# Expert query panels as three products of rounded operands, and the last searches moved beside the U blocks

## The chip, the cores and the metric

The kernel runs on one core of one Trainium2 chip. The metric is device time in microseconds (us); the kernel before has a median of 2666.05 us over three runs (2664.07 to 2666.25).

## The reference, cut to what matters

Two blocks are applied to x (256 tokens, 1024 wide). The second has two layers, and each ends with an expert layer, `peer`. Everything is float32.

```python
def peer(h, w_q, subkeys, u_tab, v_tab):             # 8 heads, 128 keys a side, top 16, 128*128 experts
    q = (xb @ w_q).reshape(128, 8, 256)
    s1 = einsum('phd,nd->phn', q[..., :128], subkeys[0])
    s2 = einsum('phd,nd->phn', q[..., 128:], subkeys[1])
    v1, i1 = top_k(s1, 16);  v2, i2 = top_k(s2, 16)
    cand = v1[..., :, None] + v2[..., None, :]       # 256 candidates a head
    cs, ci = top_k(cand, 16);  g = softmax(cs)
    e = i1[ci // 16] * 128 + i2[ci % 16]
    a = gelu(einsum('pd,phkd->phk', xb, u_tab[e]))
    return einsum('phk,phkd->pd', g * a, v_tab[e])
```

xb is the normed and modulated activation, `rmsnorm(x, g) * (1 + scale) + shift`.

## The kernel before, in words

Activations lie transposed: features on the partitions in 8 blocks (`KT`) of 128, the 256 tokens as columns. Weights come through a ring of four 1 MB slots (`ring`), one panel per slot, in the order of `SECTIONS`. SyncE issues each load (`load`, L343) once the panel that used the slot before is done with, counted on the semaphore which the section names.

An expert layer (`peer` on each engine) has these stages.

**The norm.** The 4 panels of the projection before it make 8 tiles; VectorE adds each to `xT` (`residual`, L1543), ScalarE squares it (L1036), TensorE sums the squares (`norm`, L483). After the root, VectorE scales the 8 blocks (L1534) and ScalarE adds the shift (L1048), which gives `hP`. ScalarE then rounds all of `hP` to float32r (L1075, `h_split[0]`) and VectorE computes the rest (L1630, `h_split[1]`).

**The query stage.** There are 8 panels of `peer_wq`, one per head. For each head TensorE makes two tiles (the two key sides) of 8 float32 products, weights straight from the ring (`proj_cols`, L499), and ScalarE copies each tile to `qT` (`evac`, L1029). Banks 4 and 5 alternate. One head later TensorE multiplies that head's `qT` with the subkeys (`keys`, L618) into one of banks 0 to 3, and VectorE searches them: `pick(h, tt)`, for each half of the tokens, finds the 16 best of 128 for both key sides (`first8`, `next8`, L1641 to L1661). `keys` of head h waits until the search that used its bank before has let go of it. `keys` of head 7 comes after the first U block; its two searches come in the passes b = 2 and 3 of VectorE's loop over the blocks.

**The U blocks.** All 16384 experts' U rows are multiplied with the activation, in 128 blocks (`BLOCKS`) of 128 experts. ScalarE rounds a block (`hi_u`, L1088) and VectorE computes the rest (`lo`, L1729), both into `t_split`, which lies over ring slots 2 and 3; the U panels (two blocks each) use slots 0 and 1. TensorE makes three products for each of the 8 feature blocks (`hidden`, L637): rounded by rounded, rounded by rest, rest by rounded. Only the last 8 of the 24 need VectorE's part. ScalarE rounds block b once block b-2 has been multiplied; the slot of a panel is loaded again once VectorE has finished its second block (semaphore `split`, L369).

Beside the blocks VectorE ranks the candidates in steps (`rank`): for each half of the tokens four pairs of `cand` (sums, first 8) and `rest` (next 8), `place`, six `where`, `gates`. A table written from sizes puts them at passes b: they begin at `FIRST` = 4 and spread over `SPAN` = 45 blocks. From `HOT_AT` = FIRST + SPAN + 6 = 55 each of 64 passes makes one-hot rows for four tokens, TensorE multiplies them (`gates`, L649), and from `GATE_AT` = 57 ScalarE and VectorE merge the result with the block outputs in the arena.

**The V blocks.** The same number of blocks, with products of 512 columns (L678).

Three lines fix the places that the change touches (L252, L297, L306):

```python
queries = [(a["peer_wq"][l], 8, "proj", 2)]
H_PEER = (5, 8)
FIRST, SPAN = 4, 45
```

Of the kernel before, what the change touches and what calls it, by code (L numbers as in the profile page):

```python
# [14 lines left out]
D, T, P, KT = 1024, 256, 128, 8  # L15
# [3 lines left out]
RING = 4  # L19
SLOT = 2048  # L20
EXPERTS, PH, TOPK = 16384, 8, 16
# [89 lines left out]
def build(nc, a, out):  # L111
# [4 lines left out]
    with ctx:  # L116
# [40 lines left out]
        def slot(n):  # L157
            return ring[:, n % RING, :]
# [10 lines left out]
        def kt(ap, k=KT):  # L169
# [9 lines left out]
                  "mod_acc", "mod_turn", "mod_bank", "proj", "turn", "bank4", "bank5", "sq", "ms", "var", "std", "h",  # L179
                  "h_hi", "h_split", "hi", "split", "lb", "gate", "gates_f", "logf", "expo", "exps", "lin_in",  # L180
                  "scores", "masked", "dstate", "state", "o_sum", "o_bank0", "o_bank1", "osq", "oms", "ovar", "ostd",
# [69 lines left out]
        def peer_sections(l):  # L251
            queries = [(a["peer_wq"][l], 8, "proj", 2)]  # L252
            return queries + [((a["peer_u"][l], a["peer_v"][l]), 2 * PAIRS, None, 0)]
# [25 lines left out]
        for dram, panels, signal, _ in SECTIONS:  # L279
            if dram is a["w_down"]:  # L280
                DOWN += range(n, n + panels)
            n += panels if signal is not None else 0

        LOADS_BEFORE, PROJ_BEFORE, loads, n = [], [], [0, 0], 0
        projs = 0
        for _, panels, signal, per in SECTIONS:
            projs += panels * per * (signal == "proj") + 2 * PAIRS * (signal is None)
# [41 lines left out]
        def _(sync):  # L329
# [5 lines left out]
            n, freed, layer = 0, [], 0  # L335
            total = {"proj": 0, "mod_acc": 0, "rows": 0}
            at = {}
# [12 lines left out]
            for dram, panels, signal, per in SECTIONS:  # L350
                if signal is not None:
                    k0 = at.get(id(dram), 0)
                    at[id(dram)] = k0 + panels
                    for k in range(panels):
                        total[signal] += per
                        freed.append((signal, total[signal]))
                        load(dram[k0 + k])
                    continue
# [54 lines left out]
        def _(pe):  # L413
# [186 lines left out]
            def peer(l):  # L600
# [40 lines left out]
                def gates(g):  # L641
# [8 lines left out]
                    last.then_inc(sems["g_mm"], 1)  # L650

                for h in range(PH):
                    proj_cols(1, lambda k: hP[:, k, :], T, first=(h == 0))
                    if h:
                        keys(h - 1, 3)
                pe.wait_ge(sems["h_split"], l + 1)
                for b in range(BLOCKS):
                    for tt in range(2):
                        if b == STEP_AT[tt, "gates", 0] + 2:
                            turn_routes(tt)  # L660
                    hidden(b % 2)
                    if b == 0:
                        keys(PH - 1, 2)
                    g = group_of(b, HOT_AT)
                    if g is not None:
                        gates(g)
# [350 lines left out]
        def _(act):  # L1017
# [54 lines left out]
            def peer(l, scale_col, shift):  # L1072
                norm(xT, hP, shift, "proj")
                act.wait_ge(sems["h"], H_PEER[l] * KT)
                A(h_split[:, 0, :, :], hP, ACT.Copy).then_inc(sems["h_hi"], 1)  # L1075
                qT = M5["qT"].rearrange("p (s t) -> p s t", s=16)
# [45 lines left out]

                def squares(g):
# [16 lines left out]
                for b in range(1, BLOCKS + 2):  # L1140
# [12 lines left out]
                    if g is not None:  # L1153
                        squares(g)
                    if b >= 2:
# [303 lines left out]
        def _(dve):  # L1459
# [79 lines left out]

            def residual(name, gate, mods_behind=()):  # L1540
                for k in range(KT):
                    bank, free = ring_tile(name)
                    STT(xT[:, k, :], bank[:, 0:T], modc[:, gate + k:gate + k + 1], xT[:, k, :], MUL, ADD).then_inc(free, 1)  # L1543
                    if k in mods_behind:
                        used(1)
                        mod_between(1, 16)
                dve.wait_ge(*e.tile_out())

# [75 lines left out]
            iota16 = iota[:, 0:16].unsqueeze(1).broadcast_to([P, P, 16])  # L1624

            def peer(l):
# [25 lines left out]
                def next8(rows):  # L1652
# [7 lines left out]
                    ins.then_inc(sems["dve_step"], 1)  # L1660
                    e.step()  # L1661

                def pick(h, tt):
# [109 lines left out]
                for b in range(BLOCKS + 3):  # L1773
                    if 2 <= b < BLOCKS:
# [449 lines left out]
            e.tiles("turn", 16)  # L2224
            residual("proj", 16)
            used(8)
# [112 lines left out]
```

## Time and profile before

| | |
|---|---|
| median of 3 runs | 2666.05 us |
| profiled execution, own time | 2666.74 us |
| its span, first to last instruction | 2664.9 us |
| around the span | 1.84 us |
| TensorE busy | 2585.9 us (97%) |
| VectorE busy | 1712.7 us (64%) |
| ScalarE busy | 1172.0 us (44%) |
| mean granted TensorE clock | 0.975 of 2.4 GHz |

Times of trace rows are in us from the start of the span. A float32 product is recorded as two instructions, so a tile of 8 such products shows 16; a product of float32r operands is one. Layer 0's query stage lies between 771 and 834 us, layer 1's between 1795 and 1860. A wait in brackets is the idle time of the engine before the row, with what ended it.

### The profile page before, as it was taken

The numbers are of one execution on the slowest core, as the hardware profiler recorded it, in microseconds if no ns is written. First come the engines' busy times: TensorE is split into PE (matmuls) and PEld (weight loads), VectorE is DVE, ScalarE is ACT, GpSimd is POOL, SyncE is SP. The second block draws the span as 40 slices with busy tenths as digits, with TensorE's granted clock in tenths as the row PEclk, the third lists the DMA queues.
The fourth block names the chain that finished last, engine by engine and source line by source line (L and its number), as shares of the span: only waits on it lengthen the run. The fifth ranks groups of instructions, "written<-read, shape, count | busy, mean of one in ns | idle before, by whom it ended". The sixth has DMA issues, their size and how long they took to land.

```text
span 2664.9 us, 41646 instructions
## 1 busy us (share of the span) xinstructions
PE 2585.9 (97%) x15364; PEld 2286.4 (86%) x15364; DVE 1712.7 (64%) x3469; ACT 1172.0 (44%) x2355; POOL 3.5 (0%) x10
## 2 busy tenths in 40 slices
PE   8999999999999999999999998999999999999997
PEld 4588888897889999999888887778999999888886
DVE  3662644446438977787688875536996778555554
ACT  2322010124212558776444444231557777455554
POOL 0000000000000000000000000000000000000000
PEclk9999999998999999999999999779999999999998
DMA  6562557754433554444677764212554444555553
GB/s 257 189 238 84 204 190 264 253 175 163 169 127 119 185 178 148 137 141 158 242 274 274 281 235 148 79 64 97 175 188 159 143 143 137 180 190 196 196 189 110
DMA packets 65346, 471.60 MB, mean 177 GB/s; under 512 B 7297, under 2 KB 7553, under 8 KB 8241
## 3 DMA queue, kind: packets, MB, share of 16 engines
q1 hardware_dynamic: 64656, 467.85, 50.0%
q8 instruction: 101, 1.65, 0.3%
q10 hardware_dynamic: 272, 1.05, 0.1%
q0 software_dynamic: 272, 0.69, 0.1%
q14 instruction: 45, 0.36, 0.0%
HBM read 468.51 MB, written 1.05 MB: 176 GB/s over the span
## 4 chain that ended last, share of the span: by engine, by line
PE 94%; DVE 4%; ACT 1%; issue 1%; DMA 1%; SPq 0%; DVEq 0%
PE bank L637 26%; PE bank L678 26%; PE bank L499 16%; PE bank L649 4%; PE bank L744 4%; PE bank L828 2%; PE bank L509 2%; PE bank L934 2%; PE bank L483 1%; PE bank L445 1%; PE bank L891 1%; DVE macc L1501 1%; PE bank L515 1%; PE bank L742 1%; PE bank L469 1%
## 5 line engine op out<-in xcount | busy, mean ns | idle before, releaser
L637 PE MATMUL bank<-h_split,t_split 128*128 128x256 f32 x6144 | 771.7, 285 | 4.5 <-DVE t_split L1729 4.2
L637 PEld LDWEIGHTS bank<-h_split,t_split 128*128 128x128 f32 x6144 | 745.4, 191 | 6.5 <-DVE t_split L1729 5.2
L1729 DVE TENSOR_TENSOR t_split<-ring,t_split 128x1024 fp32r<-128x1024 f32 x512 | 624.9, 1222 | 159.0 <-ACT t_split L1088 155.3
L678 PE MATMUL bank<-t_split,w_split 128*128 128x512 f32 x3072 | 703.9, 390 | 0.0
L678 PEld LDWEIGHTS bank<-t_split,w_split 128*128 128x128 f32 x3072 | 574.9, 188 | 118.7
L1093 ACT ACTIVATE t_split<-ring 128x1024 fp32r<-128x1024 f32 x256 | 271.7, 1061 | 357.9 <-PE bank L678 282.9
L1088 ACT ACTIVATE t_split<-ring 128x1024 fp32r<-128x1024 f32 x256 | 271.1, 1059 | 298.3 <-PE bank L637 264.8
L1029 ACT ACTIVATE arena<-bank 128x256 f32<-128x256 f32 (+2 forms) x160 | 64.4, 405 | 482.1 <-PE bank L499 292.4
L499 PE MATMUL bank<-H,ring 128*128 128x256 f32 (+1 forms) x960 | 246.9, 419 | 6.4 <-ACT H L1048 4.0
L1761 DVE TENSOR_TENSOR w_split<-arena,w_split 128x256 fp32r<-128x256 f32 x256 | 108.9, 425 | 223.1 <-ACT w_split L1095 223.1
L499 PE MATMUL bank<-arena,ring 128*128 128x256 f32 x1024 | 231.0, 385 | 12.2 <-ACT arena L1048 8.0
L499 PEld LDWEIGHTS bank<-H,ring 128*128 128x128 f32 x960 | 186.0, 195 | 61.1 <-issue 36.9
L499 PEld LDWEIGHTS bank<-arena,ring 128*128 128x128 f32 x1024 | 195.6, 193 | 40.7 <-issue 9.4
L1501 DVE SCALAR_TENSOR_TENSOR macc<-ring,cact,macc 128x256 f32<-128x256 f32 x336 | 162.9, 485 | 12.0
L1095 ACT ACTIVATE w_split<-arena 128x256 fp32r (+1 forms) x256 | 102.7, 401 | 0.0
L744 PE MATMUL bank<-H,ring 128*128 128x256 f32 x448 | 100.5, 381 | 0.3 <-DVE macc L1994 0.3
L744 PEld LDWEIGHTS bank<-H,ring 128*128 128x128 f32 x448 | 83.8, 190 | 11.8 <-issue 0.5
L1817 DVE SCALAR_TENSOR_TENSOR macc<-arena,cact,macc 128x256 f32<-128x256 f32 x168 | 81.1, 483 | 3.4
L1114 ACT ACTIVATE arena<-bank 128x256 f32<-128x256 f32 (+31 forms) x236 | 75.0, 318 | 0.1
L828 PE MATMUL bank<-hf_split,wd_split 128*128 128x256 f32 x528 | 66.4, 290 | 3.8 <-DVE wd_split L2043 3.8
L828 PEld LDWEIGHTS bank<-hf_split,wd_split 128*128 128x128 f32 x528 | 65.8, 198 | 4.0 <-DVE wd_split L2043 4.0
L1543 DVE SCALAR_TENSOR_TENSOR xT<-bank,modc,xT 128x256 f32<-128x256 f32 x40 | 18.8, 483 | 76.7 <-PE bank L499 64.6
(290 smaller groups left out, 2380.7 us busy)
## 6 DMA issues: line engine op xcount, KB each, us to landing
ring<-in_peer_u SPq DMA_DIRECT2D x128, 1024.0 KB, 5.0
ring<-in_peer_v SPq DMA_DIRECT2D x128, 1024.0 KB, 4.9
ring<-in_w_mod SPq DMA_DIRECT2D x24, 1024.0 KB, 5.1
ring<-in_mod_w SPq DMA_DIRECT2D x24, 1024.0 KB, 5.0
arena<-in_mod_w SPq DMA_DIRECT2D x24, 1024.0 KB, 6.6
ring<-in_w_in SPq DMA_DIRECT2D x22, 1024.0 KB, 5.0
ring<-in_w_up SPq DMA_DIRECT2D x22, 1024.0 KB, 5.1
ring<-in_peer_wq SPq DMA_DIRECT2D x16, 1024.0 KB, 4.9
```

Source lines behind the costliest of these rows:

```text
L499: last = mm(bank[:, 0:width], w[:, k, j * P:(j + 1) * P], rhs(k), start=(k == 0), stop=(k == ks - 1))
L637: last = mm(bank[:, 0:T], u[:, a_, k, :], h_split[:, b_, k, :], start=(k == 0 and a_ + b_ == 0), stop=(k == KT - 1 and a_ == 1))
L649: last = mm(BK[6 + b][:, j * P:(j + 1) * P], P2[b][:, j, :], P1[b][:, j, :], start=True, stop=True)
L678: last = mm(BK[2 * tt + hf][:, :], w_split[:, j, a_, tt * P:(tt + 1) * P], t_split[:, 1 - j, b_, hf * 512:(hf + 1) * 512], start=(first an ...
L744: last = mm(bank[:, 0:T], w[:, k, half], Hx[:, k, :], start=(k == 0), stop=(k == KT - 1))
L828: return mm(BK[d // 2][:, d % 2 * T:(d % 2 + 1) * T], w[:, j, d * P:(d + 1) * P], hf_split[:, b_, 2 * n + j, :], start=(n == j == a_ == b_ ...
L1088: A(t_split[:, 1 - j, 0, :].rearrange("p (k c) -> p k c", k=KT), ring[:, r, :].rearrange("p (k j c) -> p j k c", k=KT, j=2)[:, j], ACT.Cop ...
L1093: A(t_split[:, 1 - j, 0, :].rearrange("p (k c) -> p k c", k=KT), ring[:, r, :].rearrange("p (j k c) -> p j k c", k=KT, j=2)[:, j], ACT.Cop ...
L1095: A(w_split[:, j, 0, :], arena[:, bass.ds(at * T, T)], ACT.Copy).then_inc(sems["w_hi"], 1)
L1501: ins = STT(acc, w[:, k, :], cact[:, c_col + k:c_col + k + 1], acc, MUL, ADD)
L1729: TT(t_split[:, 1 - j, 1, :].rearrange("p (k c) -> p k c", k=KT), ring[:, r, :].rearrange(view, k=KT, j=2)[:, j], t_split[:, 1 - j, 0, :]. ...
L1761: TT(w_split[:, b % 2, 1, :], arena[:, bass.ds(at * T, T)], w_split[:, b % 2, 0, :].bitcast(f32), SUB).then_inc(sems["w_ready"], 1)
```

## The change

The query panels of both layers are handled as the U blocks are. ScalarE rounds each panel in two halves (`hi_q`), VectorE computes the rest in two halves (`lo_q`), both into `q_split`, a double buffer at the start of the arena, and TensorE makes three products (`query`). The ring slot is free once `lo_q` has read it. The rounding of the activation moves into the norm's last step: ScalarE's shift writes `h_split[0]`, and VectorE computes `h_split[1]` block by block. The rounding of heads 0 and 1 is done during the projection before the norm. `keys` of head 6 moves behind U block 0, that of head 7 behind U block 5; the searches of heads 5, 6 and 7 are cut into twelve quarters (`quarter`: one key side of one half of the tokens), one in each of the passes b = 1 to 12, and the ranking starts at block 13 and is spread over 43 blocks. `FIRST, SPAN = 13, 43` puts `HOT_AT` at 62 and `GATE_AT` at 64. In `part(j, a_, b_, ...)`, j is the tile, a_ = 1 takes the panel's rest and b_ = 1 the activation's.

```diff
-            queries = [(a["peer_wq"][l], 8, "proj", 2)]
+            queries = [(a["peer_wq"][l], PH, "q_lo", 1)]
...
+        q_split = nc.alloc_sbuf_tensor_at("q_split", [P, 2, 2, SLOT], f32r, offset=arena_at)
+        AHEAD = PH - 3
-        H_PEER = (5, 8)
+        H_PEER = (4, 7)
-        FIRST, SPAN = 4, 45
+        FIRST, SPAN = 13, 43
...
 # TensorE, peer
+                def query(h):
+                    w = q_split[:, h % 2, :, :].rearrange("p s (k c) -> p s k c", k=KT)
+                    banks = []
+                    def part(j, a_, b_, first, last_one):
+                        if first:
+                            banks.append(ring_bank())
+                        for k in range(KT):
+                            if h == j == a_ == 0:
+                                fresh(k, 1, "h_lo" if b_ else "h")
+                            last = mm(banks[j][:, 0:T], w[:, a_, k, j * P:(j + 1) * P], h_split[:, b_, k, :],
+                                      start=(first and k == 0), stop=(last_one and k == KT - 1))
+                        if last_one:
+                            last.then_inc(sems["proj"], 1)
+                    pe.wait_ge(sems["q_hi"], 2 * (PH * l + h + 1))
+                    if h == 0:
+                        pe.wait_ge(sems["q_lo"], PH * l + 1)
+                        for j in range(2):
+                            part(j, 0, 0, True, False)
+                            part(j, 1, 0, False, False)
+                        for j in range(2):
+                            part(j, 0, 1, False, True)
+                    else:
+                        for j in range(2):
+                            part(j, 0, 0, True, False)
+                            part(j, 0, 1, False, False)
+                            if j == 0:
+                                pe.wait_ge(sems["q_lo"], PH * l + h + 1)
+                            part(j, 1, 0, False, True)
...
                 for h in range(PH):
-                    proj_cols(1, lambda k: hP[:, k, :], T, first=(h == 0))
-                    if h:
+                    query(h)
+                    if 1 <= h <= AHEAD + 1:
                         keys(h - 1, 3)
-                pe.wait_ge(sems["h_split"], l + 1)
                 for b in range(BLOCKS):
...
                     if b == 0:
-                        keys(PH - 1, 2)
+                        keys(PH - 2, 4)
+                    if b == 5:
+                        keys(PH - 1, 7)
 # ScalarE, peer
-                norm(xT, hP, shift, "proj")
-                act.wait_ge(sems["h"], H_PEER[l] * KT)
-                A(h_split[:, 0, :, :], hP, ACT.Copy).then_inc(sems["h_hi"], 1)
+                def hi_q(h):
+                    m = QUERY[l][h]
+                    act.wait_ge(sems[f"loaded{m % RING}"], 16 * (m // RING + 1 + (PAIRS * l if m % RING < 2 else 0)))
+                    for j in range(2):
+                        half = slice(j * D, (j + 1) * D)
+                        A(q_split[:, h % 2, 0, half], slot(m)[:, half], ACT.Copy).then_inc(sems["q_hi"], 1)
+                if l == 0:
+                    act.wait_ge(sems["o_done"], 1 + 8)
+                hi_q(0)
+                hi_q(1)
+                squares(xT, hP, "proj")
+                std_root()
+                for k in range(KT):
+                    act.wait_ge(sems["hs"], e.more("hs"))
+                    A(h_split[:, 0, k, :], hP[:, k, :], ACT.Identity, bias=modc[:, shift + k:shift + k + 1]).then_inc(sems["h"], 1)
...
+                        act.wait_ge(sems["q_lo"], PH * l + 6)
                         hi_u(0)
                     evac("proj", qT[:, s, :], ACT.Copy)
+                    if s % 2 and s // 2 + 2 < PH:
+                        hi_q(s // 2 + 2)
+                act.wait_ge(sems["q_lo"], PH * (l + 1))
 # VectorE, peer
-                dve.wait_ge(sems["h_hi"], e.more("h_hi"))
-                TT(h_split[:, 1, :, :], hP, h_split[:, 0, :, :].bitcast(f32), SUB).then_inc(sems["h_split"], 1)
+                for k in range(KT):
+                    dve.wait_ge(sems["h"], H_PEER[l] * KT + k + 1)
+                    STT(h_split[:, 1, k, :], hP[:, k, :], modc[:, 24 + k:25 + k], h_split[:, 0, k, :].bitcast(f32), ADD, SUB
+                        ).then_inc(sems["h_lo"], 1)
...
-                for h in range(PH - 2):
+                lo_q(l, 2)
+                for h in range(AHEAD):
+                    lo_q(l, h + 3)
                     for tt in range(2):
                         pick(h, tt)
-                for tt in range(2):
-                    lo(0, tt, "p (k j c) -> p j k c")
-                    pick(PH - 2, tt)
+                lo(0, 0, "p (k j c) -> p j k c")
...
-                    if b in (2, 3):
-                        pick(PH - 1, b - 2)
+                    if b <= 12:
+                        quarter(AHEAD + (b - 1) // 4, (b - 1) // 2 % 2, (b - 1) % 2)
 # VectorE, the residual before each expert layer
-            residual("proj", 16)
+            residual("proj", 16, (), {5: lambda: lo_q(0, 0), 6: lambda: lo_q(0, 1)})
```

The loop over the blocks on VectorE now begins at b = 1 with `lo` of block 1 (before, `lo` of blocks 0 and 1 stood between the searches of head 6). `quarter` does `first8` and `next8` for one row set, and lets go of the bank after its second key side.

## Rows read from the trace of the kernel before

**Rows 1.** The page: busy time, and the chain that ended last, by line

```profile
PE 2585.9 (97%) x15364; PEld 2286.4 (86%) x15364; DVE 1712.7 (64%) x3469; ACT 1172.0 (44%) x2355; POOL 3.5 (0%) x10
PE bank L637 26%; PE bank L678 26%; PE bank L499 16%; PE bank L649 4%; PE bank L744 4%; PE bank L828 2%; PE bank L509 2%; PE bank L934 2%; PE bank L483 1%; PE bank L445 1%; PE bank L891 1%; DVE macc L1501 1%; PE bank L515 1%; PE bank L742 1%; PE bank L469 1%
```

**Rows 2.** Timeline, all engines: norm and first two heads; columns start, us, engine

```profile
763.45 0.48 DVE L1543 SCALAR_TENSOR_TENSOR xT<-bank,modc,xT 128x256 f32<-128x256 f32 x1 [2.97 <-PE bank L499]
769.67 3.26 DVE L1534 SCALAR_TENSOR_TENSOR arena<-xT,gain,nrm 128x256 f32<-128x256 f32 x8
770.19 3.30 ACT L1048 ACTIVATE arena<-arena,modc 128x256 f32<-128x256 f32 x8 [2.34 <-DVE arena L1534]
770.84 15.49 PE L499 MATMUL bank<-arena,ring 128*128 128x256 f32 x64 [3.98 <-ACT arena L1048]
...
1795.40 16.90 PE L499 MATMUL bank<-arena,ring 128*128 128x256 f32 x64 [3.98 <-ACT arena L1048]
```

**Rows 3.** Windows around that start: PE, PEld, DVE, ACT, POOL busy, then granted clock

```profile
772.00:773.00 1.00, 1.00 (x4) 0.82 (x3) 0.92 (x3) 1.00 (x4) 0.00 (x0) 0.50 0.00 0
774.00:775.00 1.00, 1.00 (x7) 0.87 (x6) 0.00 (x0) 1.00 (x1) 0.00 (x0) 1.00 0.00 0
1800.00:1801.00 1.00, 1.00 (x4) 0.82 (x3) 0.97 (x1) 0.00 (x0) 0.00 (x0) 0.50 0.00 0
```

**Rows 4.** Timeline, layer 0, one head of the query stage in its steady part

```profile
817.37 1.05 PE L618 MATMUL bank<-small,arena 128*128 128x128 f32 x8
818.01 0.50 DVE L1644 MAX8 arena<-bank 128x8 f32<-128x128 f32 x2 [2.17 <-PE bank L618]
820.80 0.48 DVE L1644 MAX8 arena<-bank 128x8 f32<-128x128 f32 x2
821.91 0.38 ACT L1029 ACTIVATE arena<-bank 128x256 f32<-128x256 f32 x1 [3.96 <-PE bank L499]
825.17 1.05 PE L618 MATMUL bank<-small,arena 128*128 128x128 f32 x8
```

**Rows 5.** Timeline of ScalarE, steady U blocks: the rounding of two successive blocks

```profile
866.77 1.06 ACT L1088 ACTIVATE t_split<-ring 128x1024 fp32r<-128x1024 f32 x1 [1.55 <-PE bank L637]
869.65 1.06 ACT L1088 ACTIVATE t_split<-ring 128x1024 fp32r<-128x1024 f32 x1 [1.55 <-PE bank L637]
```

**Rows 6.** Timeline of TensorE, first U blocks of layer 0

```profile
833.78 3.12 PE L637 MATMUL bank<-h_split,t_split 128*128 128x256 f32 x24
...
849.36 3.13 PE L637 MATMUL bank<-h_split,t_split 128*128 128x256 f32 x24 [0.78 <-DVE t_split L1729]
853.99 46.21 PE L637 MATMUL bank<-h_split,t_split 128*128 128x256 f32 x381 [1.50 <-DVE t_split L1729]
```

**Rows 7.** Windows of the U blocks, columns as in Rows 3

```profile
845.00:857.00 12.00, 9.73 (x77) 9.12 (x77) 11.76 (x40) 3.99 (x6) 0.00 (x0) 1.00 0.42 133
857.00:869.00 12.00, 12.00 (x103) 12.00 (x102) 11.79 (x34) 5.32 (x8) 0.00 (x0) 1.00 0.62 220
1872.00:1884.00 12.00, 10.11 (x82) 9.70 (x81) 11.79 (x37) 3.99 (x6) 0.00 (x0) 1.00 0.51 171
```

**Rows 8.** Timeline of VectorE among the ranking steps

```profile
864.98 1.23 DVE L1729 TENSOR_TENSOR t_split<-ring,t_split 128x1024 fp32r<-128x1024 f32 x1
866.12 0.75 DVE L1685 TENSOR_TENSOR arena<-arena 128x256 f32<-128x256 f32 x2
869.40 1.23 DVE L1729 TENSOR_TENSOR t_split<-ring,t_split 128x1024 fp32r<-128x1024 f32 x1
871.95 0.75 DVE L1655 MAX8 arena<-arena 128x8 f32<-128x256 f32 x2
873.62 1.23 DVE L1729 TENSOR_TENSOR t_split<-ring,t_split 128x1024 fp32r<-128x1024 f32 x1
```

**Rows 9.** Groups by line, VectorE, 846 to 983 us: a `where` step

```profile
L1710 DVE TENSOR_TENSOR arena<-arena,con 128x2048 f32<-128x2048 f32 x4 | 9.1, 2286 | 0.0
```

**Rows 10.** The page: DMA issues, KB each, us from issue to landing

```profile
ring<-in_peer_u SPq DMA_DIRECT2D x128, 1024.0 KB, 5.0
```

More of the change, by code:

```diff
@@ L282, in build @@
             n += panels if signal is not None else 0
+        QUERY, n = [], 0
+        for _, panels, signal, _ in SECTIONS:
+            if signal == "q_lo":
+                QUERY.append(range(n, n + panels))
+            n += panels if signal is not None else 0
         LOADS_BEFORE, PROJ_BEFORE, loads, n = [], [], [0, 0], 0
@@ L286, in build @@
         for _, panels, signal, per in SECTIONS:
-            projs += panels * per * (signal == "proj") + 2 * PAIRS * (signal is None)
+            projs += panels * (2 if signal == "q_lo" else per * (signal == "proj")) + 2 * PAIRS * (signal is None)
             if signal is None:
@@ L335, in _ @@
             n, freed, layer = 0, [], 0
-            total = {"proj": 0, "mod_acc": 0, "rows": 0}
+            total = {"proj": 0, "mod_acc": 0, "rows": 0, "q_lo": 0}
             at = {}
@@ L355, in _ @@
                         total[signal] += per
+                        if signal == "q_lo":
+                            total["proj"] += 2
                         freed.append((signal, total[signal]))
@@ L650, in gates @@
                     last.then_inc(sems["g_mm"], 1)
+                def query(h):
[26 more added lines that the diff above has]
+                            part(j, 1, 0, False, True)
+                    e.skip(f"loaded{panel[0] % RING}", 16)
+                    panel[0] += 1
                 for h in range(PH):
-                    proj_cols(1, lambda k: hP[:, k, :], T, first=(h == 0))
-                    if h:
+                    query(h)
+                    if 1 <= h <= AHEAD + 1:
                         keys(h - 1, 3)
-                pe.wait_ge(sems["h_split"], l + 1)
                 for b in range(BLOCKS):
@@ L1121, in stored, with offsets @@
                       ).then_inc(sems["g_store"], 1)
-                def squares(g):
+                def offsets(g):
                     if g >= 2:
@@ L1153, in peer @@
                     if g is not None:
-                        squares(g)
+                        offsets(g)
                     if b >= 2:
@@ L1538, in norm, with residual @@
                     ins.then_inc(sems["h"], KT)
-            def residual(name, gate, mods_behind=()):
+            def residual(name, gate, mods_behind=(), also={}):
                 for k in range(KT):
@@ L1546, in residual @@
                         mod_between(1, 16)
+                    if k in also:
+                        also[k]()
                 dve.wait_ge(*e.tile_out())
@@ L1624, in _, with lo_q @@
             iota16 = iota[:, 0:16].unsqueeze(1).broadcast_to([P, P, 16])
+            def lo_q(l, h):
+                for j in range(2):
+                    half = slice(j * D, (j + 1) * D)
+                    dve.wait_ge(sems["q_hi"], 2 * (PH * l + h) + j + 1)
+                    ins = TT(q_split[:, h % 2, 1, half], slot(QUERY[l][h])[:, half], q_split[:, h % 2, 0, half].bitcast(f32), SUB)
+                ins.then_inc(sems["q_lo"], 1)
             def peer(l):
@@ L1661, in next8, with quarter @@
                     e.step()
+                def quarter(h, tt, half):
+                    n = 2 * h + tt
+                    bank, free = BK[n % 4], sems[f"rank_bank{n % 4}"]
+                    dve.wait_ge(sems["ranked"], RANKS * l + n + 1)
+                    rows = [(bank[:, half * P:(half + 1) * P], s2[:, half * P:(half + 1) * P],
+                             topv[:, tt, h, half, :], topi[:, tt, h, half, :])]
+                    if half:
+                        first8(rows).then_inc(free, 1)
+                        dve.wait_ge(free, (5 if n % 4 < 2 else 4) * l + n // 4 + 1)
+                    else:
+                        first8(rows).then_inc(sems["dve_step"], 1)
+                        dve.wait_ge(sems["dve_step"], e.stepped())
+                    next8(rows)
                 def pick(h, tt):
@@ L1765, in peer @@
                 used(8)
-                for h in range(PH - 2):
+                lo_q(l, 2)
+                for h in range(AHEAD):
+                    lo_q(l, h + 3)
                     for tt in range(2):
                         pick(h, tt)
-                for tt in range(2):
-                    lo(0, tt, "p (k j c) -> p j k c")
-                    pick(PH - 2, tt)
+                lo(0, 0, "p (k j c) -> p j k c")
                 e.tiles("proj", 16)
-                for b in range(BLOCKS + 3):
-                    if 2 <= b < BLOCKS:
+                for b in range(1, BLOCKS + 3):
+                    if b < BLOCKS:
                         lo(b // 2 % 2, b % 2, "p (k j c) -> p j k c")
-                    if b in (2, 3):
-                        pick(PH - 1, b - 2)
+                    if b <= 12:
+                        quarter(AHEAD + (b - 1) // 4, (b - 1) // 2 % 2, (b - 1) % 2)
                     if b >= 3:
@@ L2224, in _ @@
             e.tiles("turn", 16)
-            residual("proj", 16)
+            residual("proj", 16, (), {5: lambda: lo_q(1, 0), 6: lambda: lo_q(1, 1)})
             used(8)
```

2 lines of the change are left out of this document (1 added, 1 removed).

## The prediction

> **What bounds the kernel now.** I read the page first: TensorE is busy 97% of the span, and of the chain that ended last 16% is float32 products of L499, the line that the query panels use too [rows 1]. So time is saved only where TensorE has less to do or stands less. Then the timelines of the stage. A tile of 8 float32 products takes 3.45 us (a residual row and the wait before it, 0.48 + 2.97) [rows 2], so a panel of two takes 6.90. From one head's `keys` to the next is 825.17 - 817.37 = 7.80 us, so `keys` costs 0.90. In that period VectorE needs 2 x 2.79 = 5.6 us for two searches (from one MAX8 to the next) and waits 2.17 us [rows 4]. The stage runs from 770.84 [rows 2] to the first U block at 833.78 [rows 6], 62.9 us; in layer 1 the first four tiles take 1.4 us longer [rows 2]. In the U blocks TensorE goes on without a gap, one block of 24 products every 869.65 - 866.77 = 2.88 us, 0.120 us a product [rows 5]. It stands only near the start, where VectorE is late with `lo` [rows 6]: in the 12 us of the first window 77 products begin where the undisturbed window has 103, in layer 1's worst window 82 [rows 7]. At 0.120 us that is 3.1 and 2.5 us lost.
>
> **TensorE's query panels.** 48 products of 0.120 us are 5.76 us a panel, where 6.90 go; the operands and shapes are those of a U block. The bounds for the price of a product are 0.117 (12 us by the 103 of the full window [rows 7]) and 0.130 (3.12 by 24, which holds a drain [rows 6]). Seven panels save 7 x 1.14 = 8.0 us a layer.
>
> The first panel is special. The activation's blocks come 0.41 us apart (3.30 by 8) and ScalarE has written the last 2.65 us after TensorE starts (773.49 - 770.84) [rows 2]. The first tile's 8 products go at that pace, and nothing behind them may pass; with a hand-over and the last product at the low clock they end at 3.1 us, and the panel takes 3.1 + 40 x 0.120 = 7.9 us. Before, the first two panels took 15.49 us, the first thus 8.6 [rows 2]. TensorE has stood 3.98 us for the norm and begins at a clock of 0.50; it is 1.00 by 774 in layer 0, while layer 1 still has 0.50 at 1800 [rows 3], 4.6 us after its start. I let the clock return at the same moments: nothing more in layer 0, and half of 2.6 us, 1.3, in layer 1, against 1.4 before. The first panel thus gives 0.7, and 0.8 in layer 1.
>
> **The other engines in the stage.** ScalarE's rounding of a panel is 2 x 1.06 us [rows 5] and follows the evacuation of the head two earlier, so it is done 2.6 us after that head's end; TensorE needs it 6.65 us after it. VectorE's `lo` takes 1.14 us until the next instruction starts (866.12 - 864.98) [rows 8], a panel 2.28, and with two searches 7.86 us a head. TensorE's head is 5.76 + 0.90 = 6.66. VectorE is thus the slower one and falls 1.2 us behind per head; moving three heads' searches out is what ends that. Counted from the end of head 1's products: the rest of panel 3 is done at 2.6 + 1.1 = 3.7, then one search pair and one panel each 7.86, so panels 4 to 7 at 11.6, 19.4, 27.3, 35.1. TensorE starts head h at 0.9 + 6.66 (h - 2) and wants the rest after 16 products, 1.9 later: 16.1, 22.8, 29.4, 36.1. The spare falls to 1.0 us at head 7. Head 7 ends at 0.9 + 33.3 + 5.8 = 40.0; U block 0 wants `lo` at 41.9 and has it at 35.1 + 5.6 + 1.2 = 41.9. Nothing is lost, and 0.2 us more a head on VectorE would cost up to 1. What a bank holds back (`keys` of head 5 needs the searches of head 3) is free by 33, before 34.
>
> The stage thus lasts 7.9 + 5.8 + 40.0 = 53.7 us, 9.2 less than 62.9. One `keys` (0.90) has moved into the U blocks and comes off: **8.3 us in layer 0, 8.4 in layer 1**.
>
> **What I cost at nothing.** `hi_q` of heads 0 and 1 lies ahead of the squares on ScalarE: panel 1 lands some 5 us [rows 10] after the second projection panel is free, with four tiles still to come, and 8 squares catch up before TensorE wants them. If that cover went, the norm would be late by what is missing, up to 2 us. `lo_q` of heads 0 and 1 is 2.28 us in VectorE's waits of 2.97 [rows 2]; it fits. VectorE's parts of the activation follow ScalarE's block by block and are wanted only after 32 products. The removed full-width roundings lay beside TensorE's work. Ring loads start earlier than before, since a slot is free at `lo_q`; the first U panels wait for heads 5 to 7, 5 us before they are used at the latest.
>
> **The U blocks.** A quarter is half of a 2.79 us search, 1.4, to 2.8 if the halves shared everything; I take 1.5, because only the hand-overs between dependent steps are shared. With `lo` that is 2.65 us per block against TensorE's 2.88, and TensorE has two `keys` more there: VectorE starts even and stays so. Before, it started with three searches owed, which gave the 3.1 and 2.5 us; those go. Next late is the ranking. It is denser: `cand` 3.28 (869.40 - 866.12) and `rest` 1.67 (873.62 - 871.95) [rows 8] four times, six `where` of 2.3 [rows 9], and some 2 for the rest make 35.7 us per half, 71.4 over 43 blocks, 1.66 a block; with `lo` 2.80 against 2.88. And the table puts `cand`, `rest`, `cand` at blocks 13, 14 and 15: 3 x 1.14 + 8.4 = 11.9 us in 8.6. The debt of 3.2 meets an ease of 2.4 (`lo` is normally done 1.1 + 1.2 us after the previous block's start and wanted at 2.88 + 1.92, so 2.4 later): 0.9 us lost per layer, with 0 to 3 as bounds. The last gates come at block 125 instead of 118, and V's first rounding waits for them; TensorE has blocks 126 and 127 meanwhile, so 0, up to 1.
>
> **Sum.** 8.3 + 8.4 + (3.1 + 2.5) - 2 x 0.9 = 20.5 us. Against the profiled execution's 2666.74 this gives 2646.2; it lies 0.7 above the median of 2666.05, which gives **2645.5**.
>
> **Rivals.**
> (A) The forecast: 60%.
> (B) VectorE becomes the bound in the query stage: a panel and two searches cost 8.5 instead of 7.86 (contention, a hand-over before each `lo_q`). For it: a spare of only 1.0 us at head 7. Against: all its parts have rows. Four heads late by 0.6 and the same debt at blocks 0 to 5 cost 2.5 to 5 us per layer: 2651 to 2655. 17%.
> (C) The clock returns later in the first panel, because its products come 0.41 us apart and leave TensorE waiting between them where float32 products at the low clock filled it. If all of a first panel's 40 remaining products ran at 0.50, that is 4.8 us a layer, less 1.3: up to 8.3, so 2649 to 2654. For it: layer 1 kept the low clock 4.6 us at full work [rows 3]. 13%. The Trainium skill (TensorE: Matmul & The Clock Gate, Part 1) calls the halved clock the resting state, which activity releases; by that rule thin work keeps it low.
> (D) The other side: a product pays its weight load in the open. 48 loads a panel take the place of 32 instructions (two per float32 product). Nearest row: a key instruction with 128 columns costs 0.90 / 8 = 0.11 us. At 0.120 + 0.11 a panel is 11 us and 768 products add 85: 2730. It decides from 0.120 + 20.5 / 768 = 0.147 us a product. Against it stand the U blocks with the same form at 0.120 [rows 5]. 4%. The Trainium skill (the same page, Part 3, The mechanism) says a weight load overlaps with running matmuls only when its row group differs; every load here takes all rows, so by that rule D would hold, and rows 5 speak against it.
> (E) The change does not do what it says, since the early waits and the ranking give back what the panels save (a U panel that lands late in each pair of blocks of the denser ranking, 0.2 us a block over 43 blocks and two layers is 17 us): about 2662. For it: VectorE at 97% there. 6%.
>
> **How the numbers follow.** About 0.2%, 5.3 us, is what a measurement of this kernel tells from no change. A, B and C are faster by more, E partly: faster 0.93; within: 0.03; slower, D and a bad E: 0.04. The range takes A with its bounds (0.117 a product gives 2 us more, no ranking stall 1.8 more, clock in layer 1 1 more: 2640) and B and C up to 2655.
>
> **What would show it.** Query products at 0.120 us, heads 6.66 us apart, first U block some 53.7 us after the first query product. VectorE waits of 2.17 us before searches gone, its `lo` of panel 7 about 1 us before TensorE wants it. No TensorE wait in blocks 1 to 12, one of about 1 us near block 16. Low clock gone by the same moments. I am wrong in the main step if a head's products take over 6.2 us, in VectorE's if TensorE waits for `lo_q`, and in the U blocks if waits for VectorE there add to more than 4 us a layer.

## The result, and the profile after

The changed kernel takes 2643.72 us (median of 4 runs, 2640.44 to 2647.02) where the kernel before takes 2666.15 (4 runs): a ratio of 0.9916, 95% interval 0.9897 to 0.9934. The forecast was 2645.5 and the range 2639 to 2655. The profiled execution took 2647.02 us with a span of 2645.2, 19.7 less than the span of before.

The page of the changed kernel: busy time, the chain that ended last by engine and by line, and the new group of query products.

```profile
PE 2566.3 (97%) x15620; PEld 2281.5 (86%) x15620; DVE 1751.9 (66%) x3501; ACT 1194.1 (45%) x2385; POOL 3.5 (0%) x10
PE 89%; DVE 8%; ACT 1%; issue 1%; DMA 0%; DVEq 0%; SPq 0%
PE bank L724 26%; PE bank L647 26%; PE bank L509 11%; PE bank L659 4%; PE bank L790 4%; PE bank L874 2%; PE bank L519 2%; PE bank L980 2%; PE bank L674 1%; DVE macc L1565 1%; PE bank L455 1%; PE bank L937 1%; PE bank L493 1%; PE bank L525 1%; DVE q_split L1697 1%
L674 PE MATMUL bank<-h_split,q_split 128*128 128x256 f32 x768 | 101.3, 293 | 8.0 <-ACT h_split L1135 8.0
```

TensorE is as full as before (97%, [rows 1]) and has less to do. Float32 products (now L509) fell from 16% of the chain to 11%, and VectorE's work on `q_split` has come in with 1%. The two waits of L674, 8.0 us in all, are those for the norm.

The same line by engine, in the page of the kernel before:

```profile
PE 94%; DVE 4%; ACT 1%; issue 1%; DMA 1%; SPq 0%; DVEq 0%
```

VectorE's share of the chain has doubled, from 4% to 8%.

The timeline of TensorE in layer 0 of the changed kernel: start, us, then the group; in brackets a wait.

```profile
770.06 15.35 PE L674 MATMUL bank<-h_split,q_split 128*128 128x256 f32 x96 [3.98 <-ACT h_split L1135]
785.25 1.05 PE L628 MATMUL bank<-small,arena 128*128 128x128 f32 x8
...
791.75 1.05 PE L628 MATMUL bank<-small,arena 128*128 128x128 f32 x8
...
818.54 5.88 PE L674 MATMUL bank<-h_split,q_split 128*128 128x256 f32 x48
824.26 2.08 PE L647 MATMUL bank<-h_split,t_split 128*128 128x256 f32 x16
827.09 1.22 PE L647 MATMUL bank<-h_split,t_split 128*128 128x256 f32 x8 [0.76 <-DVE t_split L1820]
...
876.00 24.26 PE L647 MATMUL bank<-h_split,t_split 128*128 128x256 f32 x200 [0.81 <-DVE t_split L1820]
```

Against [rows 4] the heads are 6.50 us apart (791.75 - 785.25), not 7.80. Less the 0.89 of `keys` (a `keys` group starts 0.89 us before the products behind it in the timeline with float32 panels below), a panel's 48 products take 5.61 us, 0.117 each. Against [rows 6] the waits for VectorE in the U blocks have moved from blocks 4 to 6 to block 0 (0.76) and block 16 (0.81).

Where the time went can be added up from the first query product, the first U product and the first V product of the two executions:

| us | before | after | difference |
|---|---|---|---|
| layer 0, query stage | 62.94 | 54.20 | -8.74 |
| layer 0, U blocks | 430.27 | 430.11 | -0.16 |
| layer 1, query stage | 64.35 | 54.55 | -9.80 |
| layer 1, U blocks | 430.27 | 430.05 | -0.22 |

That is 18.9 of the 19.7 us of the spans. Layer 0's stage begins 0.8 us earlier, which is not the work of the new panels: it does so too in x1 below, with float32 panels (770.02). The stretch from layer 0's V blocks to layer 1's first query product differs by 1 us one way, the end by 1 us the other. The differences of the U blocks are no larger than those between two executions of the changed kernel (430.11 and 430.51 us in layer 0).

The first head is the odd one. It ends at 785.25 less a panel of 5.61, so it took 9.6 us, and the granted clock says why. Windows of the changed kernel, columns as in [rows 3]:

```profile
772.00:774.00 2.00, 2.00 (x9) 1.78 (x8) 2.00 (x6) 0.71 (x2) 0.00 (x0) 0.50 0.00 0
776.00:777.00 1.00, 1.00 (x7) 1.00 (x7) 0.00 (x0) 0.00 (x0) 0.00 (x0) 0.50 0.00 0
778.00:779.00 1.00, 1.00 (x11) 1.00 (x10) 0.00 (x0) 0.09 (x1) 0.00 (x0) 1.00 0.00 0
1792.00:1793.00 1.00, 1.00 (x6) 1.00 (x6) 0.00 (x0) 0.00 (x0) 0.00 (x0) 0.50 0.00 0
1795.00:1797.00 2.00, 2.00 (x19) 2.00 (x18) 0.00 (x0) 0.61 (x2) 0.00 (x0) 1.00 0.00 0
```

Before, the 2.4 GHz were back by 774 in layer 0 [rows 3]; now, with the stage beginning 0.8 us earlier, 776 still shows 0.50 (1.2 GHz), and the clock is back 7 to 8 us after the first query product in both layers. Six or seven products begin in 1 us at 0.50, eleven at 1.00.

### The profile page after: what moved, and what is told of

Read it like the earlier page. It is cut to its first block, busy times and chain, and to the rows that moved or that the text cites. A ratio compares the mean times of both kernels' runs of the same rounds, so it can differ in the third digit from the quotient of the medians.

```text
span 2645.2 us, 42222 instructions
## 1 busy us (share of the span) xinstructions
PE 2566.3 (97%) x15620; PEld 2281.5 (86%) x15620; DVE 1751.9 (66%) x3501; ACT 1194.1 (45%) x2385; POOL 3.5 (0%) x10
## 3 DMA queue, kind: packets, MB, share of 16 engines
q10 hardware_dynamic: 272, 1.05, 0.1%
HBM read 468.51 MB, written 1.05 MB: 178 GB/s over the span
## 4 chain that ended last, share of the span: by engine, by line
PE 89%; DVE 8%; ACT 1%; issue 1%; DMA 0%; DVEq 0%; SPq 0%
PE bank L724 26%; PE bank L647 26%; PE bank L509 11%; PE bank L659 4%; PE bank L790 4%; PE bank L874 2%; PE bank L519 2%; PE bank L980 2%; PE bank L674 1%; DVE macc L1565 1%; PE bank L455 1%; PE bank L937 1%; PE bank L493 1%; PE bank L525 1%; DVE q_split L1697 1%
## 5 line engine op out<-in xcount | busy, mean ns | idle before, releaser
L1075 ACT ACTIVATE arena<-bank 128x256 f32<-128x256 f32 (+2 forms) x160 | 64.3, 405 | 451.7 <-PE bank L509 194.4
L509 PE MATMUL bank<-H,ring 128*128 128x256 f32 (+1 forms) x960 | 244.6, 416 | 6.5 <-ACT H L1094 4.0
L509 PEld LDWEIGHTS bank<-H,ring 128*128 128x128 f32 x960 | 185.0, 194 | 59.6 <-issue 35.7
L509 PE MATMUL bank<-arena,ring 128*128 128x256 f32 x512 | 113.7, 381 | 4.2 <-DVE H L2108 2.2
L509 PEld LDWEIGHTS bank<-arena,ring 128*128 128x128 f32 x512 | 96.3, 190 | 18.3 <-DVE H L2108 3.0
L674 PE MATMUL bank<-h_split,q_split 128*128 128x256 f32 x768 | 101.3, 293 | 8.0 <-ACT h_split L1135 8.0
L674 PEld LDWEIGHTS bank<-h_split,q_split 128*128 128x128 f32 x768 | 97.0, 197 | 10.5 <-issue 8.7
L1178 ACT ACTIVATE arena<-bank 128x256 f32<-128x256 f32 (+32 forms) x250 | 79.9, 320 | 0.1
```

What stands on the lines that cost most here:

```text
L509: last = mm(bank[:, 0:width], w[:, k, j * P:(j + 1) * P], rhs(k), start=(k == 0), stop=(k == ks - 1))
L674: last = mm(banks[j][:, 0:T], w[:, a_, k, j * P:(j + 1) * P], h_split[:, b_, k, :], start=(first and k == 0), stop=(last_one and k == KT - 1))
```

## The experiments

**One part each.** The first kernel has the searches, `keys` and ranking of the changed one and the panels of the one before. The second is the reverse.

```diff
 # x1, from the kernel before
-        FIRST, SPAN = 4, 45
+        FIRST, SPAN = 13, 43
...
+                    if b <= 12:
+                        quarter(AHEAD + (b - 1) // 4, (b - 1) // 2 % 2, (b - 1) % 2)
 # x2, from the changed kernel
-        FIRST, SPAN = 13, 43
+        FIRST, SPAN = 4, 45
...
-                for h in range(AHEAD):
-                    lo_q(l, h + 3)
+                for h in range(PH - 2):
+                    if h + 3 < PH:
+                        lo_q(l, h + 3)
```

> The searches, keys and ranking placed as in the changed kernel, the query panels still float32 products and rounding of the activation as before. My theory (the panels' products carry the gain, moving searches alone buys only the removed waits at the first U blocks): stage about 62.0 us from the first query product to the first U block (62.9 less one keys), waits for VectorE in the U blocks 0.8 us a layer instead of 2.3, one keys more there; in all 1.5 us a layer, 2663 us. Rival (VectorE was what held the stage, so moving searches is the gain): heads under 7.8 us apart and 2655 us or less.

> The three products, with the searches of heads 5 to 7 and the ranking placed as in the kernel before. My theory (VectorE with 7.8 us a head against TensorE's 6.5 then becomes the bound at the end of the stage): heads still 6.5 us apart, but U block 0 waits about 4.7 us for VectorE, and 2.3 us more are lost in blocks 3 to 6; 5.4 us a layer above the changed kernel, about 2654 us. Rival (the ring and the banks have ease enough, VectorE's debt is hidden): within 2 us of the changed kernel, 2644 to 2646 us.

Measured: x1 takes 0.9988 of the kernel before (0.9979 to 0.9998, 2661.75 against 2665.16 us), x2 takes 0.9989 (0.9979 to 0.9998, 2661.69). The timeline of TensorE in x1, then in x2:

```profile
825.89 1.05 PE L619 MATMUL bank<-small,arena 128*128 128x128 f32 x8
826.78 7.07 PE L500 MATMUL bank<-arena,ring 128*128 128x256 f32 x32
833.50 3.21 PE L638 MATMUL bank<-h_split,t_split 128*128 128x256 f32 x24
...
884.40 20.80 PE L638 MATMUL bank<-h_split,t_split 128*128 128x256 f32 x171 [0.81 <-DVE t_split L1747]
```

```profile
816.70 5.90 PE L674 MATMUL bank<-h_split,q_split 128*128 128x256 f32 x48
823.42 2.15 PE L647 MATMUL bank<-h_split,t_split 128*128 128x256 f32 x16
830.78 2.08 PE L647 MATMUL bank<-h_split,t_split 128*128 128x256 f32 x8 [5.22 <-DVE t_split L1818]
832.66 1.91 PE L628 MATMUL bank<-small,arena 128*128 128x128 f32 x8
```

x1 went as my theory had it: with float32 panels VectorE's searches, 5.6 us a head [rows 4], are hidden (heads stay 7.80 us apart), and what changes is the waits in the U blocks, to one of 0.81 for VectorE near block 16 (layer 1 has another, of 1.21, for ScalarE). Its stages of 63.48 and 63.38 us are 1.4 above my figure, since the clock was back only after 6 us in both. x2 went further than both theories. The panels are as fast as in the changed kernel (stages of 54.97 and 54.84 us with one `keys` more), but U block 0 waits 5.2 us for VectorE, and the U blocks last 437.9 and 438.4 us, 7.8 and 8.4 more than the changed kernel's. In layer 0 the rows give (5.22 + 0.38 + 1.49) - (0.76 + 0.81) - 0.89 for the `keys` that is not there = 4.6 of the 7.8. Most of the other 3.2 is what the wait does to the clock, which my 5.4 lacked: TensorE runs at 0.50 for 5.7 us behind the wait, which costs half of that, 2.8. Windows of x2:

```profile
826.00:828.00 2.00, 0.00 (x0) 0.00 (x0) 1.93 (x13) 0.00 (x0) 0.00 (x0) 1.00 0.00 0
830.00:831.00 1.00, 0.22 (x1) 0.22 (x2) 1.00 (x3) 0.00 (x0) 0.00 (x0) 0.50 0.00 0
834.00:835.00 1.00, 1.00 (x6) 1.00 (x6) 1.00 (x3) 1.00 (x1) 0.14 (x1) 0.50 0.00 0
```

TensorE stands, the clock falls to 0.50, and the `keys` behind the wait take 1.91 us instead of 1.05. So a wait of 5.2 us there costs about 8. Alone, the two parts bring 3.4 and 3.5 us, where both together bring 22 (19 in the repeat below): each makes the other worth having.

**The first head.** Two edits on the changed kernel. The fill gives TensorE four products with each block of the activation instead of one. The warm-up puts nine float32 products of constants into its wait for the norm; their result is used by nothing.

```diff
 # x3: the fill
-                        for j in range(2):
-                            part(j, 0, 0, True, False)
-                            part(j, 1, 0, False, False)
+                        banks += [ring_bank(), ring_bank()]
+                        for k in range(KT):
+                            fresh(k, 1, "h")
+                            for j in range(2):
+                                for a_ in range(2):
+                                    mm(banks[j][:, 0:T], w[:, a_, k, j * P:(j + 1) * P], h_split[:, 0, k, :],
+                                       start=(k == a_ == 0), stop=False)
 # x5: the warm-up
+        WARM = 9
...
                 norm(hP)
+                for _ in range(WARM):
+                    mm(BK[3][:, 0:T], ones, C("scan_g"), start=True, stop=True)
```

> Head 0's products are reordered: with each block of the activation as it comes, four products (both tiles, rounded and rest of the panel) instead of one. Theory thin work (the clock comes back late in the changed kernel because TensorE waits between its first products): the clock is back 3 to 6 us after the first product instead of 7 to 7.7, and head 0 takes 7.4 to 8.5 us instead of 9.7; 1.5 to 2.3 us a layer, about 2640 us. Rival theory chance (the moment at which the clock returns is not tied to how thin the first products are): it is back 7 us after the first product as now, and only the filled waits are saved, 0.5 to 1 us a layer, about 2642 us.

> Nine float32 products of constants (result unused) fill TensorE's 4 us wait for the norm ahead of each query stage. If the halved clock in head 0 comes from that wait: granted clock 1.00 from the first query product, head 0 takes 7.5 us instead of 9.7 to 10, 2.2 to 2.5 us a layer gained, about 2639 us. If the clock falls for another reason, or the fill makes the first query product late: clock still 0.50 or head 0 unchanged, 2644 us or more.

Windows of x3, then of x5, in layer 0 and layer 1:

```profile
771.00:773.00 2.00, 2.00 (x11) 2.00 (x11) 2.00 (x7) 2.00 (x6) 0.00 (x0) 0.50 0.67 283
774.00:775.00 1.00, 1.00 (x11) 1.00 (x10) 1.00 (x4) 0.00 (x0) 0.00 (x0) 1.00 0.00 0
1784.00:1785.00 1.00, 1.00 (x11) 1.00 (x10) 1.00 (x4) 0.00 (x0) 0.00 (x0) 0.99 0.00 0
```

```profile
771.00:773.00 2.00, 1.94 (x6) 0.93 (x5) 2.00 (x6) 2.00 (x7) 0.00 (x0) 1.00 0.76 320
774.00:776.00 2.00, 2.00 (x12) 2.00 (x11) 2.00 (x6) 0.00 (x0) 0.00 (x0) 0.50 0.03 8
1791.00:1793.00 2.00, 2.00 (x20) 2.00 (x19) 1.24 (x4) 0.00 (x0) 0.00 (x0) 1.00 0.00 0
```

In x3 the stages begin at 770.58 and 1779.95, so the clock is back 3 to 4 us after the first product, not 7; the stages last 51.71 and 52.15 us, 2.5 and 2.4 less than the changed kernel's. In x5 the clock is up when the stage begins (770.81), but in layer 0 it falls at about 774, after 3 us in which TensorE got one product with each block of the activation; in layer 1 it stays up. The stages last 53.79 and 52.37 us. The medians of these two cannot tell this (2643.51 and 2644.51 us, 4 runs each, which spread over 4 to 6 us); the traces can. Between the two stages the executions differ by as much as the edits bring: from layer 0's first V product to layer 1's first query product x3's took 527.1 us and the changed kernel's 532.4. In one of two stages thin work lowered the clock with no long wait before it.

**Two waits on VectorE.** The rest of U block 0 goes ahead of the last search, and the table's `cand` size becomes 36.

```diff
-                 for p in range(4) for part, size in (("cand", 33), ("rest", 18))]
+                 for p in range(4) for part, size in (("cand", 36), ("rest", 18))]
...
                     for tt in range(2):
+                        if h == AHEAD - 1 and tt == 1:
+                            lo(0, 0, "p (k j c) -> p j k c")
                         pick(h, tt)
-                lo(0, 0, "p (k j c) -> p j k c")
```

> The rest of U block 0 is taken ahead of the last search of the stage, and the ranking table is given a cand size of 36, so that its first steps fall in blocks 13, 15 and 16 instead of 13, 14 and 15. My theory (both waits of TensorE in the changed kernel's U blocks are order on VectorE, 0.76 at block 0 and 0.81 at block 16): both gone, U stage 1.5 us shorter in each layer, 2641 us. Rival (VectorE is at its limit there and the waits come back a few blocks later): waits of the same sum at other blocks, 2644 us.

Measured: 2640.06 us (4 runs, 2636.09 to 2645.44, too wide a spread to show a gain of this size). Both waits are gone in both layers; the timeline of TensorE in layer 0 shows one stretch from block 6 to block 31, across block 16:

```profile
824.48 3.03 PE L647 MATMUL bank<-h_split,t_split 128*128 128x256 f32 x24
...
843.43 75.34 PE L647 MATMUL bank<-h_split,t_split 128*128 128x256 f32 x624
919.13 8.89 PE L647 MATMUL bank<-h_split,t_split 128*128 128x256 f32 x72 [0.36 <-ACT arena L1178]
```

The U blocks last 428.81 and 429.10 us, 1.3 and 1.0 less. A wait for ScalarE's evacuation has come in near block 32 (0.36, and 0.66 in layer 1). ScalarE itself had stood 3.4 us for a U panel that landed late. Timelines of x6, VectorE and ScalarE:

```profile
903.42 1.23 DVE L1820 TENSOR_TENSOR t_split<-ring,t_split 128x1024 fp32r<-128x1024 f32 x1
906.88 1.22 DVE L1820 TENSOR_TENSOR t_split<-ring,t_split 128x1024 fp32r<-128x1024 f32 x1
...
917.75 1.06 ACT L1148 ACTIVATE t_split<-ring 128x1024 fp32r<-128x1024 f32 x1 [3.37 <-DMA ring<-in_peer_u]
918.71 0.36 ACT L1178 ACTIVATE arena<-bank 128x256 f32<-128x256 f32 x1
```

Beside the `where` steps VectorE's rests start 3.46 us apart, against TensorE's 2.88 a block, and a slot is loaded again only when VectorE has read it. So both theories hold in part, mine for the larger one: 0.36 of 1.57 us (0.66 of 1.51 in layer 1) came back some blocks later, by way of the ring. That VectorE's pace is what made this panel late is read from the rows; no run changed it.

**Fill and warm-up together, and all four.**

> The filled start of head 0 and the constants' products in the norm's wait, together. Theory thin work (the clock falls or stays low when TensorE's first products are thin, with or without a wait before them): granted clock 1.00 through all of head 0 in both layers, 5.6 to 5.9 us for its 48 products, first U block 50 us after the first query product instead of 54.4; 8 to 9 us less than the changed kernel in the two stages, about 2635 us. Theory wait alone (the fall in layer 0 of the kernel with the fill alone was chance of the moment): the clock falls again in one of the layers, 51 to 53 us there.

> All four edits: filled start, constants' products in the norm's wait, rest of block 0 ahead of the last search, cand size 36. If they add: 50 us from first query product to first U block, no waits for VectorE in the U blocks, 12 us less than the changed kernel, about 2632 us. If VectorE becomes the bound with the shorter head 0: waits for the panels' rest at heads 6 and 7 and 2636 us or more.

x7 takes 2637.08 us (4 runs). Its clock is 1.00 throughout the first head in both layers, and its stages last 51.09 us both times. Windows and timeline of x7:

```profile
772.00:774.00 2.00, 2.00 (x17) 2.00 (x18) 2.00 (x7) 2.00 (x6) 0.00 (x0) 1.00 0.86 365
1784.00:1786.00 2.00, 2.00 (x20) 2.00 (x19) 2.00 (x6) 2.00 (x5) 0.00 (x0) 1.00 0.55 225
```

```profile
771.98 3.98 PE L690 MATMUL bank<-h_split,q_split 128*128 128x256 f32 x32
775.79 8.42 PE L677 MATMUL bank<-h_split,q_split 128*128 128x256 f32 x64
784.05 1.05 PE L631 MATMUL bank<-small,arena 128*128 128x128 f32 x8
```

My 50 us missed one wait. The first 32 products are done by 775.8, and the last 16 want VectorE's rest of the activation, which comes until 777.2 (it starts at 773.98 in x7 and takes 3.26 us). Head 0 thus takes 6.5 us (784.05 - 5.61 - 771.98), not 5.7. The two stages are 6.6 us shorter than the changed kernel's, where I had expected 8 to 9. x8 has stages of 51.11 and 51.13 us and U blocks of 429.17 and 429.95; together that is 7.5 us less than in the changed kernel, not 12, and 1.5 less than in x7. It takes 2639.2 us (6 runs, 2630.8 to 2641.5), which does not tell it from x7, and misses the 2632 of adding up. No panel's rest is waited for at heads 6 and 7, so VectorE did not become the bound.

**VectorE's spare.**

```diff
                         pick(h, tt)
+                    dve.memset(M5["eq"][:, 0:256], 0.0)
```

> VectorE writes 256 unused zeros after the searches of each of the five heads in the stage (0.2 to 0.3 us a head more). By the changed kernel's trace VectorE's rest of panel 7 is done 0.1 us before TensorE wants it, so the spare is gone: TensorE waits for it at head 6 or 7, together with block 0's wait 1.0 to 1.5 us a layer more than the changed kernel's 0.76. If the spare is the 1.0 us of the prediction: no wait for a panel's rest, and block 0 waits 1.0 us longer all the same.

The timeline of x9 at head 7:

```profile
814.10 0.27 DVE L1862 MEMSET arena<- 128x256 f32 x1
814.29 2.29 DVE L1697 TENSOR_TENSOR q_split<-ring,q_split 128x1024 fp32r<-128x1024 f32 x2
...
816.63 4.04 PE L674 MATMUL bank<-h_split,q_split 128*128 128x256 f32 x32 [0.65 <-DVE q_split L1697]
```

With 0.19 us a head more (814.29 - 814.10) TensorE waits 0.65 us for the rest of panel 7, and 0.94 at block 0, 1.6 us in all against 0.76 (1.64 against 0.71 in layer 1). Five heads by 0.19 is 0.95; 0.83 came through (0.93 in layer 1), a little under the 1.0 that I had expected. The kernel was run once, 2644.53 us, which says nothing against the changed kernel's 2640 to 2649. So the changed kernel has no spare there: VectorE's work from head 1 to block 0 is a chain of its own, as long as TensorE's.

**Changed kernel and x7 once more**, side by side with the kernel before.

> The changed kernel once more, as the measure for the next run on the same chip. Its stages as in the first trace if the clock's moments are no chance: granted clock back 6.5 to 8 us after the first query product in both layers, first U block 54 to 55 us after it. If the late return was chance: once at least back within 5 us.

> The kernel with the filled start and the constants' products once more. By its two stages, each 3.1 to 3.5 us shorter, it should be 6 to 7 us below the changed kernel of the same call, about 2637 against 2644 us. If what is gained there is given back elsewhere: within 2 us of it.

The changed kernel has 0.9927 (0.9914 to 0.9941, median 2645.05 us), x7 0.9909 (0.9896 to 0.9923, 2639.36 us): 5.7 us apart, where the stages make 6.2. The stages repeat closely: 54.02 and 54.40 us, with the clock back in the seventh and the eighth microsecond of the two, against 51.07 and 51.15.

The repeat also answers the theory of chance in x3. Windows of layer 0, of the repeat and then of x3, whose first query products come at 767.40 and 770.58:

```profile
767.00:768.00 1.00, 0.59 (x2) 0.57 (x2) 1.00 (x4) 1.00 (x4) 0.00 (x0) 0.56 1.01 426
773.00:774.00 1.00, 1.00 (x7) 1.00 (x6) 0.00 (x0) 0.00 (x0) 0.00 (x0) 0.53 0.00 0
```

```profile
770.00:771.00 1.00, 0.42 (x2) 0.45 (x3) 1.00 (x4) 1.00 (x3) 0.00 (x0) 0.63 1.01 426
773.00:774.00 1.00, 1.00 (x8) 1.00 (x7) 1.00 (x4) 0.23 (x1) 0.00 (x0) 0.67 0.00 0
```

A mean of 0.56 puts the fall at 767.1, and 0.63 puts it at 770.3: in both kernels the clock falls 0.3 us before the first product (in layer 1, 0.7 us behind it in both). It is back 6.5 us after the first product in the repeat and 3.1 in x3 (7.5 and 4.1 in layer 1). So with the fall at the same moment of the stage the fuller start has the clock back 3.4 us sooner, twice.

## Why the prediction was right

**The panels.** The main term was 7 x 1.14 = 8.0 us a layer; it measured 7 x (6.90 - 5.61) = 9.0. The price taken from the U blocks, 0.120, was a little high, and the lower bound, 0.117, was the value: a U block takes 2.88 us in the query's neighbourhood too, while a query tile of 24 products takes 2.80. The 0.08 lie in every product and not in a hand-over (in the trace the products of a query panel start 0.117 us apart, those of U block 0 0.120); why was not tried.

**The first head.** Here rival C's mechanism was at work, at less than its price (it had 3.5 to 8.3 us in all): 7.9 us forecast (9.2 in layer 1), 9.6 and 9.9 measured, 2.4 more together. The step that failed is "I let the clock return at the same moments". By the granted clock of each microsecond it came back 6.1 to 7.6 us after the first product in the ten stages with thin first products and no warm-up (the changed kernel twice, x2, x6, x9), and 3.1 and 4.1 us after it with the fill. With float32 products it was 2.9 and 5.8 us before, 6.0 and 5.8 in x1; so layer 0 of the profiled execution of before had an early return that three of the four stages with float32 panels do not have, and rival C's cost over it is part chance. With x1's return the stage before would last about 64.3 us in both layers (63.48 and the `keys` that x1 moves out), and the change then takes 10 us from each. In head 0 of layer 0 the late return took back more than the cheaper products gave (8.6 us before, 9.6 after); the stages came out at 54.2 and 54.55 us for 53.7 and 55.0. The Trainium skill (TensorE: Matmul & The Clock Gate, Part 1) says that activity releases the clock; the traces of x3 and x7 agree (back after 3.1 and 4.1 us with the fill, 1.00 all through with both).

**VectorE in the stage.** The chain was set up rightly: counted from the end of head 1's products (785.25), the rest of panel 7 was due at 35.1 us and came at 35.1. The spare was not: 1.0 us at head 7 became 0.04 (its rest is done at 820.37, TensorE wants it at 818.54 + 16 x 0.117 = 820.41), because TensorE was faster than I took it. The same error put block 0's wait at nothing where 0.76 us was measured. x9 shows that this is the edge; rival B did not happen, but 0.2 us a head would have begun it.

**The U blocks.** Predicted 0.9 us at block 16, by the table's order of `cand`, `rest`, `cand`; measured 0.81, and in x6 it is gone with another order. The closeness is part luck: by the prediction's own rows `cand`, `rest` and `cand` are 3.28 + 1.67 + 3.28 = 8.2 us and not 8.4, which leaves 0.6 of the 0.9. Mis-sized was what the change took away there: I counted missing products in a window and got 3.1 and 2.5 us, where the waits in the rows are 0.78 + 1.50 and, in layer 1, 0.38 + 0.41 + 1.48, 2.3 both. The waits as the rows name them were the better measure. With block 0's wait and the `keys` that moved in, the U blocks gave 0.2 us a layer instead of the 0.7 to 1.3 that my terms make.

**The sum, and the luck in it.** The two stages were to give 18.5 us and gave 18.5, but by errors that cancel: the panels gave 2.1 more than forecast, the first heads 2.4 less. The U blocks gave 0.4 where the terms make 2.0. The profiled executions are thus 19.7 us of span apart for a sum of 20.5. The medians are 22.4 apart here and 19.2 in the repeat, so it is chance of the executions that the measured median lies below the forecast. What I costed at nothing around the norm held: TensorE's wait for it is 3.98 us in both layers, as before.

**The rivals.** D (a weight load paid in the open) is out: 0.117 us a product, with all rows of the array in use, below the 0.147 from which it would have decided. The sentence of the Trainium skill that the prediction drew on (the same page, Part 3, The mechanism) does not describe this stream; the same section also lets a load into the background weight buffer go ahead, which would fit, but no run here tells which buffer a load takes. E did not happen. What the sum did not show is how little each half of the change brings alone.

## What to carry to other kernels

Before replacing work on the bound engine by cheaper work, lay out the next engine's work per step beside it: here VectorE's 5.6 us of searches a head were hidden under TensorE's 7.8, and with the panel's rest 7.8 us against 6.5 were not, and the move of three heads' searches is what let the panels' gain through. A wait on TensorE of some microseconds must be priced with the clock behind it (5.2 us cost about 8 here; behind the waits of 0.8 us the clock stayed at 1.00), and a start that trickles one product per arriving block should be given more to do per block and kept warm: only both together held 1.00 in all six stages tried (x7, its repeat, x8). Read waits from the rows that name them rather than from counts in a window.

## What the runs showed of the hardware

The granted clock fell from 1.00 to 0.50 in x5's layer 0 after 3 us in which TensorE got one product of 0.12 us every 0.41 us, with no longer wait in the 7 us before them; in layer 1 the same kernel kept 1.00. After a wait of 5.2 us on VectorE (x2) the clock was at 0.50 until 836.5, 5.7 us after work began again. The changed kernel's own times go with the mean clock: 2640.4 and 2640.8 us at 0.978, 2646.7 and 2647.0 at 0.975 to 0.976, and in the repeat 2640.6 at 0.978 and 2643.8 to 2648.6 at 0.976 to 0.977; where outside the query stages that clock is lost was not looked into.
